# Twelve expert weight slots instead of six, ten filled in the router, and squares added on VectorE

## The reference, cut to what matters

```python
def swiglu(xb, wg, wu, wd):
    return (jax.nn.silu(xb @ wg) * (xb @ wu)) @ wd

def hier_moe(h, lp):
    ...
    eid = grp[:, None].astype(jnp.int32) * MOE_EXPERTS_PER_GROUP + top_i.astype(jnp.int32)
    ...
    order = jnp.argsort(flat_e)
    se, st, sw = flat_e[order], flat_t[order], w.reshape(-1)[order]
    counts = jnp.bincount(flat_e, length=MOE_EXPERTS)
    ...
    yb = lax.map(expert_block, (xin, block_e)).reshape(n_rows, d)
    return jax.ops.segment_sum(yb[dest] * sw[:, None].astype(h.dtype), st, num_segments=t)

def _rms_norm(x, w):
    xf = x.astype(jnp.float32)
    y = xf * lax.rsqrt(jnp.mean(xf * xf, axis=-1, keepdims=True) + EPS)
    return (y * w.astype(jnp.float32)).astype(x.dtype)

def _swiglu(h, w1, w3, w2):
    return (jax.nn.silu(h @ w1) * (h @ w3)) @ w2
```

## Time and profile before

| | |
|---|---|
| median of 3 runs | 2530.34 us (2528.55 to 2536.39) |
| profiled execution | 2529.34 us, span 2528.0, mean granted clock 0.992 |
| busy, share of the span | PE 96%, DVE 56%, ACT 41%, POOL 12% |
| chain that ended last | PE 74%, DVE 11%, DMA 10%, ACT 4%; of DMA's, 6% is the expert tile `pair<-in_ed` |
| weight tiles of experts | 192 of 1024 KB, 9.6 to 11.8 us from issue to landing at the median |
| DMA rate in the slices of the experts | 398 to 417 GB/s |
| waits of PE, whole span | 14.6 us ahead of line 739, 11.1 ahead of 1291 |

### The profile page before, as it was taken

How to read it: one execution, slowest core, us unless ns; L and a number is a source line. 1 busy time by engine, 2 the same in 40 slices (tenths; PEclk the granted TensorE clock), 3 DMA queues, 4 the chain that set the end, 5 groups by cost and what they waited for, 6 DMA issues and landing times.

```text
span 2528.0 us, 30627 instructions
## 1 busy us (share of the span) xinstructions
PE 2426.0 (96%) x12294; PEld 1876.3 (74%) x12294; DVE 1409.5 (56%) x2043; ACT 1036.8 (41%) x1570; POOL 301.5 (12%) x256
## 2 busy tenths in 40 slices
PE   6999999999999989999999889999999999999999
PEld 4877868687877767666666678888888777888887
DVE  3676776768636676544555565334443667543442
ACT  2424333343536346544555553223343546422221
POOL 0010112112222311111111120000013000000000
PEclk9999999999999989999999999999999999999999
DMA  7324243333446259999999823232232111323322
GB/s 273 113 75 167 79 155 121 116 118 103 139 152 237 103 201 373 417 407 398 404 407 403 351 92 103 81 117 90 85 124 75 43 42 59 109 76 107 101 79 79
DMA packets 115747, 428.10 MB, mean 169 GB/s; under 512 B 16320, under 2 KB 30912, under 8 KB 89872
## 3 DMA queue, kind: packets, MB, share of 16 engines
q1 hardware_dynamic: 91488, 377.42, 41.0%
q10 hardware_dynamic: 12960, 25.17, 2.7%
q0 software_dynamic: 11152, 23.49, 2.7%
HBM read 411.60 MB, written 31.72 MB: 175 GB/s over the span
## 4 chain that ended last, share of the span: by engine, by line
PE 74%; DVE 11%; DMA 10%; ACT 4%; issue 1%; POOL 0%; SPq 0%; ACTq 0%; POOLq 0%; DVEq 0%
PE bank L739 18%; PE bank L741 18%; PE bank L740 18%; DMA pair<-in_ed 6%; PE bank L1291 3%; PE bank L1292 2%; PE bank L1293 2%; DVE HLB L280 2%; PE bank L1348 2%; DVE HLB L417 2%; ACT HLB L406 1%; PE bank L1654 1%; DMA raw<-in_wxbc 1%; DVE XGl L3002 1%; PE bank L1677 1%
## 5 line engine op out<-in xcount | busy, mean ns | idle before, releaser
L417 DVE TENSOR_TENSOR HLB<-raw,HLB 128x1024 fp32r<-128x1024 f32 (+1 forms) x286 | 346.7, 1215 | 382.1 <-ACT HLB L406 381.8
L739 PE MATMUL bank<-HTh,HLB 128*128 128x512 f32 (+1 forms) x1358 | 542.5, 400 | 14.6 <-DVE HLB L417 11.0
L741 PE MATMUL bank<-HTh,HLB 128*128 128x512 f32 (+1 forms) x1358 | 531.0, 391 | 0.0
L740 PE MATMUL bank<-HTl,HLB 128*128 128x512 f32 (+1 forms) x1358 | 528.2, 389 | 0.0
L406 ACT ACTIVATE HLB<-raw 128x1024 fp32r<-128x1024 f32 (+1 forms) x294 | 289.4, 991 | 298.9 <-PE bank L741 270.9
L739 PEld LDWEIGHTS bank<-HTh,HLB 128*128 128x128 f32 x1358 | 257.1, 189 | 97.3 <-issue 27.4
L740 PEld LDWEIGHTS bank<-HTl,HLB 128*128 128x128 f32 x1358 | 257.3, 189 | 54.0 <-issue 1.9
L741 PEld LDWEIGHTS bank<-HTh,HLB 128*128 128x128 f32 x1358 | 257.3, 189 | 53.8
L280 DVE TENSOR_TENSOR HLB<-pair,HLB 128x1024 fp32r<-128x1024 f32 x136 | 159.6, 1221 | 110.2 <-ACT HLB L271 109.4
L271 ACT ACTIVATE HLB<-pair 128x1024 fp32r<-128x1024 f32 x136 | 135.9, 1062 | 120.4 <-DMA pair<-in_ed 108.3
L741 PE MATMUL bank<-FAh,HLB 128*128 128x512 f32 x352 | 139.2, 396 | 0.0
(11 more groups left out here) (606 smaller groups left out, 4356.8 us busy)
## 6 DMA issues: line engine op xcount, KB each, us to landing
pair<-in_ed SPq DMA_DIRECT2D x64, 1024.0 KB, 11.3
raw<-in_f SPq DMA_DIRECT2D x120, 512.0 KB, 3.4
pair<-in_eg SPq DMA_DIRECT2D x47, 1024.0 KB, 9.6
raw<-in_eu SPq DMA_DIRECT2D x47, 1024.0 KB, 11.3
raw<-in_wada SPq DMA_DIRECT2D x40, 512.0 KB, 4.2
raw<-in_eg SPq DMA_DIRECT2D x17, 1024.0 KB, 11.6
pair<-in_eu SPq DMA_DIRECT2D x17, 1024.0 KB, 11.8
raw<-in_wxbc SPq DMA_DIRECT2D x24, 512.0 KB, 4.1
```

Source lines behind the costliest of these rows:

```text
L417: self.nc.vector.tensor_tensor(lo, raw, hi.bitcast(F32), ALU.subtract).then_inc(*self.w_lo.next(n))
L739: mm(bank, ah, bh, start=(start and i == 0), stop=False)
L740: mm(bank, ah, bl, start=False, stop=False)
L741: ins = mm(bank, al, bh, start=False, stop=(stop and i == n - 1))
```

## The change

The slots become twelve: beside the six of before, four `ht_pair` in the halves HTh and HTl of the normed input (no longer read once the token rows are written), `tmp_pair` in TMP[2] to TMP[5], `dec_pair` in the buffer of the decays, from which WROW moves out. A table of turns tells a tile's slot: the first five tiles go to slots 0, 1, 2, 3, 10, then the turn is 0, 1, 6, 7, 8, 9, 11, 4, 5, 2, 3, 10. SP loads two tiles as before, goes on to seven once the mean square ("square", 1) and MU_STD ("std") are done, and to twelve once PE has passed the token rows ("rows"); numbers 10 and 11 are of expert 2 and wait for `eids`.

The first four parts are split early: ACT makes two hi halves at the router's start and two behind the offsets' copies, and GpSimd, not DVE, makes their lo halves (`lo_early`, signal `x_first`). DVE's `moved(6)`, `moved(7)`, `normed(0)`, `normed(1)` come behind the slots' indices. PE's rank matmuls come ahead of the first four `offset`, its weight row and slots matmuls ahead of the first `turn_in`, which fills with one constant matmul, not three. PICK waits in addition for the last tile in `dec_pair`. The next block's first loads wait for the last tiles in slots 0, 1 and 4, now 185, 186 and 180 in place of 186, 187 and 190. ACT writes the squares of "n1" to four buffers of TMP by turns, DVE adds them, and `pe_rms` comes right behind the first product.

```diff
+        for n in range(6 * len(small)):
+            self.at.append(turns[0][n] if n < len(turns[0]) else turns[1][(n - len(turns[0])) % len(turns[1])])
+            self.before.append(had.get(self.at[n], -1))
+            had[self.at[n]] = n
+        self.last_in = had
...
     def raw(self, n):
-        return self.slots[n % len(self.slots)]
+        return self.slots[self.at[n]]
+
+    def rest(self, h):
+        return self.lo_first.when(h) if self.lo_first and h < FIRST_PARTS else self.w_lo.when(h)
+
+    def free(self, sp, n):
+
+        if n in self.first:
+            sp.wait_ge(*self.rest(self.first[n] + 1))
+        elif n >= 0:
+            sp.wait_ge(*self.pe_out.when(("tile", n)))
...
+    def lo_early(self, pool):
+
+        while self.lo_made < FIRST_PARTS:
+            h = self.lo_made
+            hi, lo, raw, _n = self.part(h)
+            pool.wait_ge(*self.w_hi.when(h))
+            self.nc.gpsimd.tensor_tensor(lo, raw, hi.bitcast(F32), ALU.subtract).then_inc(*self.lo_first.next(h))
+            self.lo_made += 1
...
+        ht_pairs = [place(f"ht_pair{i}", [128, 2048], off=HT_AT + 2048 * i) for i in range(4)]
+        tmp_pair = place("tmp_pair", [128, 2048], off=TMP_AT + 1024)
+        dec_pair = place("dec_pair", [128, 2048], off=DEC)
...
-                        keep_busy(bank, 3)
+                        keep_busy(bank, 1)
...
-            turn_in(0)
             if S.kept:
                 pe_weight_row()
                 pe_slots()
+            turn_in(0)
...
         def act_router():
+            ring.hi(act, "wr", 0, itself=True)
+            act.wait_ge(*pe_out.when(("used", ring.start_of("wr", 0))))
+            tiles.hi(act, 2)
             act.wait_ge(*pe_out.when("rcol"))
...
+            tiles.hi(act, FIRST_PARTS)
             act.wait_ge(*act_out.when("rcol"))
...
-                if i == 2:
-                    ring.hi(act, "wr", 0, itself=True)
-                    act.wait_ge(*pe_out.when(("used", ring.start_of("wr", 0))))
-                    tiles.hi(act, 4)
...
-                act_square("n1", k)
+                if k > 3:
+                    act.wait_ge(*dve_out.when(("sumsq", "n1", max(k - 4, 1))))
+                activation(TMP[k % 4][:, :], XT[:, k, :], ACT.Square).then_inc(*act_out.next(("sq", "n1", k)))
...
-            tiles.lo(dve, 4)
-            moved(6)
-            moved(7)
-            for k in range(2):
-                normed(k)
...
+                tiles.free(dve, tiles.last_in[11])
...
+            for k in range(1, 8):
+                dve.wait_ge(*act_out.when(("sq", "n1", k)))
+                if k > 1:
+                    dve.wait_ge(*dve_out.when(("sumsq", "n1", k - 1)))
+                tensor_tensor(SQ[:, :], TMP[0][:, :] if k == 1 else SQ[:, :], TMP[k % 4][:, :], ALU.add).then_inc(
+                    *dve_out.next(("sumsq", "n1", k)))
...
+            tiles.lo_early(pool)
...
         tiles.load(sp, 2)
         sp.wait_ge(*pe_out.when(("used", ring.start_of("wo", 7))))
-        tiles.load(sp, 4)
+        sp.wait_ge(*pe_out.when(("square", 1)))
+        sp.wait_ge(*act_out.when("std"))
+        tiles.load(sp, 7)
+        sp.wait_ge(*pe_out.when("rows"))
+        tiles.load(sp, 12)
...
         for i in (0, 1, 4):
-            n = max(n for n in range(len(tiles.order)) if n % len(tiles.slots) == i)
-            sp.wait_ge(*x_lo.when(tiles.first[n] + 1))
+            tiles.free(sp, tiles.last_in[i])
```

More of the change, by code:

```diff
@@ L246, in load @@
             n = self.loaded
-            before = n - len(self.slots)
-            if before in self.first:
-                sp.wait_ge(*self.w_lo.when(self.first[before] + 1))
-            elif before >= 0:
-                sp.wait_ge(*self.pe_out.when(("tile", before)))
+            self.free(sp, self.before[n])
             source = self.source(*self.order[n])
@@ L254, in load @@
             self.nc.sync.dma_start(self.raw(n).rearrange("p (k n) -> p k n", k=k), source).then_inc(
[L255 removed]
+                *self.loads[self.at[n]].next(n))
             self.loaded += 1
@@ L267, in hi @@
             hi, _lo, raw, n = self.part(h)
-            act.wait_ge(*self.loads[n % len(self.slots)].when(n))
+            act.wait_ge(*self.loads[self.at[n]].when(n))
             if h >= NHL:
@@ L292, in whole @@
         n = self.tile_of[(j, name, a)]
-        pe.wait_ge(*self.loads[n % len(self.slots)].when(n))
+        pe.wait_ge(*self.loads[self.at[n]].when(n))
         return n, self.raw(n).rearrange("p (k n) -> p k n", k=k)
@@ L1217, in pe_router @@
                 rows(2, q)
-            for i in range(2):
-                for q in range(2):
-                    offset(i, q)
             bank = psum.take(pe, "rank")
@@ L1226, in pe_router @@
             psum.give("rank", dve_out, "rk")
+            for i in range(2):
+                for q in range(2):
+                    offset(i, q)
             for q in range(2):
@@ L3025, in dve_experts @@
                 dve_slots()
+                for k in (6, 7):
+                    moved(k)
+                for k in range(2):
+                    normed(k)
             for j in range(len(blocks)):
```

41 lines of the change are left out of this document (22 added, 19 removed).

## The result

The changed kernel takes **2513.2 us** (median of 5 runs, 2512.26 to 2518.85), the kernel before 2533.2 (2528.55 to 2537.41) in the same measurement: a ratio of **0.993**, 95% interval 0.9918 to 0.9942. That is 20.0 us between the medians, where the prediction had 18.5, and 2513.2 lies within its range. The interval of the ratio reaches from 14.7 to 20.8 us, and the profiled execution, of 2515.06 us, has a span of 2513.8, only 14.2 less than the span before. So that the two numbers agree to 1.5 us is in part luck.

What follows compares the result with a forecast made beforehand. The weight queue was taken to bound the expert stage. From the profiled 2529.34 us, 10.9 (last tile earlier), 1.5 (seam) and 6.0 (squares) come off: 2510.9, or 2511.8 us against the median; range 2501 to 2523.

Steps and rivals of the forecast that it cites:

- P: Start of PE's first expert matmul, forecast at 925.7 us, 4.4 later than the 921.35 before.
- The hold: Router, ahead of the rank matmuls: GpSimd's lo-half operations hold up DVE's mask chain by 6.6 us (0 to 10.4).
- The clock: Router, behind the rank wait: PE's clock falls after standing 6.4 us, adding 2.5 us (0 to 3.4).
- The last write of token rows: Router: only 0.8 us (0 to 2) was added, for tiles 7 to 9 in the stretch around the gather.
- They run while the gather flies and cost nothing: Router: PE's weight row and slots matmuls, now ahead of the transposes, add 0 us to P.
- From P to the last landing: Expert stage: last weight tile lands at P+500.5 (P+515.7 before), with tile 22 at P+38.9, then 2.70 us a tile.
- Ten early tiles: Weight queue: how many of ten are early decides little, as the queue stands some 5.5 us before tile 22.
- Seam: Behind the experts: the next block's first loads go out ahead of expert 30's scatter, saving 1.5 us (0 to 3).
- Squares: Next block's mean square: VectorE adds the squares, PE's wait and low clock go, saving 6.0 us (3.45 to 6.3).
- No hold-up: Rival, router: DVE isn't held up by GpSimd, P is 917.6, total 2503.7 us; chance 0.20.
- Gathers behind the tiles: Rival, expert stage: more queued tiles delay gathers and scatters, so PE lags, total 2519.5 us; chance 0.20.
- A slower queue: Rival, weight queue: more slots slow the tiles; at 2.85 us a tile the total is 2537.3 us; chance 0.07.

Runs made afterwards that it cites:

- n1pool: Changed kernel with the next block's squares summed on GpSimd again and pe_rms back inside PE's long product: 2522.6 us, ratio 0.9961.
- seam: Changed kernel with the next block's first loads held again until tile 190 is split: 2517.8 us, ratio 0.9950.
- fill: Changed kernel with eight constant matmuls on PE ahead of its wait for the rank masks: 2507.7 us, ratio 0.9905.
- seven: Changed kernel with tiles 7 to 9 loaded behind the first gather, seven tiles early in place of ten: 2518.6 us, ratio 0.9949.
- dvelo_six: Changed kernel with the four early splits on DVE at other places, tile 6 in an ht_pair slot, six tiles early: 2506.5 us, ratio 0.9895.
- best1: dvelo_six with first turn_in ahead of weight row and slots matmuls, five constant matmuls before first transposes, tiles 6 to 9 right behind the gather's landing: 2502.7 us.
- eight: Changed kernel with eight slots in place of twelve, ten tiles early all the same: 2529.9 us, ratio 0.9988.
- later: Changed kernel with GpSimd's four early splits waiting until DVE has made the rank masks: 2510.6 us, ratio 0.9913.
- best2: best1 with two constant matmuls on PE ahead of the last expert's down matmuls: 2498.6 us, ratio 0.9875.

## Why the prediction was right, and where it was not

**What bounds the kernel.** Right: the weight queue, before and after. PE is busy for 271.79 of 280 us now and is no bound; it waits 0.5 us for a raw tile and 8.0 for halves from 1120 to the end of the experts.

**P.** Wrong by 14.1 us, of which 1.3 lie ahead of the router; counted from MU_STD 12.8, and 9.8 and 10.3 in n1pool and seam. The hold was sized right (6.5 for 6.6), and so was the order of events. The size is luck in part: two and a half operations of GpSimd were a choice between 0 and 10.4 us, for a chain of two-input operations, and of the four that were held three have one input. Three steps failed.
- The clock. I gave it 2.5 us, 3.4 at the most, from ten us behind another wait. It lasted from the rank to the blocks matmuls, all of the path: 22.8 us in place of 12.2 in this profile, 18.9 to 19.7 in five others with the same router, 11.9 in fill. Less the 12.2 of the forecast the term is 6.7 to 10.6 us.
- The last write of token rows. The sum had 0.8 us for the early tiles beside the gather. They stood beside the write ahead of it, which took 8.8 us for 3.1, and the gather came 7.0 us behind the blocks matmuls, not 3.7 (3.6 in seven, without those tiles). The prediction followed the queue past the gather's issue and not past what the gather waits for.
- "They run while the gather flies and cost nothing", of the weight row and slots matmuls. They, at the low clock, and the wait ahead of them take the time from 926.6 to 934.6, which the late write hid here; without that write, dvelo_six has P 11.5 us behind its gather, best1 9.1.

**From P to the last landing.** Wrong by 9.0 us, to the other side. Tile 22 came at P+37.7 for P+38.9. The 170 tiles from there to the last landing took 453.8 us (977.44 to 1431.22), not 461.6: 2.67 us a tile with the first landing, and in the chain 31.4 us a pair (six pairs from 1163.46 to 1351.95) where I held on to 32.4. In n1pool the 170 tiles take 454.1 us, but tile 22 comes at P+40.6, so there it is 5.8 us, not 9.0: the 7.8 of the rate repeat, the 1.2 at tile 22 don't. The assumption that the rate doesn't depend on depth was called the one that would be most wrong, and it was, with a sign that the prediction did not price: it had a slower queue as a rival and no faster one. The dips that it could have read were in the trace of before, in the rate by slices, behind a share of 1.01.

The two errors cancelled: 12.8 late at P, 9.0 gained behind it. Neither was foreseen, so that the sum came out is luck. The last landing was 5.0 us later than predicted, of which 1.3 again lie ahead of the router.

**Ten early tiles.** That fewer would cost nothing isn't contradicted by seven's profile, and not shown by its times. The stand of the queue that it rests on is there: DMA's share is 0.11 from 974 to 976 in the changed kernel, 1.00 in seven. eight shows that ten early ones without the slots bring little.

**Seam.** Forecast 1.5, up to 3. From the down matmuls to the transposes of the results (1456.86 before, 1448.55 now) 2.5 us were gained. The mechanism, the scatter beside the loads, was right: 6.28 us before, 2.6 now. What the traces show of its worth is 0.9 to 1.9 us: 0.9 of the 2.5 are the wait for the results (2.46 before the transposes at 1456.86, 1.56 now), 1.9 in seam, and the other 1.6 are the way from the down matmuls to PICK, 9.06 us before and 7.5 now, a clock that differs between kernels with the same instructions there.

**Squares.** Forecast 6.0. The long product starts at 1497.12 with no wait. By the same matmuls in both traces (the last one of the first product, and the fifteenth of the long one: 1503.85 and 1514.39 before, 1496.55 and 1500.72 now) it gained 10.54 - 4.17 = 6.4 us, and undoing it costs 6.3 in n1pool's profile. Right in its parts; that the medians lie 7.8 to 9.4 us apart isn't explained.

**Rivals.** No hold-up: refuted, by the rows and by later. Gathers behind the tiles: refuted, 7.6 and 9.5 us at a depth of ten. A slower queue: refuted, it is faster.

## What to carry to other kernels

A wait of TensorE is priced with what follows it: here 8.1 us of standing cost some 7 to 11 more, and the cheapest cure was work that nobody needs, put into the wait. A DMA busy share of 1.0 doesn't say that the transfers are as fast as they can be; read the rate by slices, and where it dips, more slots may bring more than the head start that they were meant for. A small operation with a busy neighbour on GpSimd and a small write behind large reads, both on the way to the critical step, cost more than their own length. And before 3 us in a stage are explained, look for another profile with the same instructions there.

## What the runs showed of the hardware

- GpSimd's operation of 128x1024 held up DVE's copies, casts, scalings, scans and two-input operations of 0.17 to 0.29 us for up to 2.4 us, the length of GpSimd's. DVE's searches for maxima (lines 2856 and 2859) beside the second split stayed at 0.37 and 0.09 to 0.16 us.
- The rate of one queue of 1 MB loads from HBM: 405, 412 and 422 GB/s at six, eight and twelve slots, at the same busy share.
- A gather's time to landing does not depend on how many tiles are queued ahead (7.3 and 9.7 us with some four, 7.6 and 9.5 with ten), while a tile's goes from some 10 to 12 us to 23 to 28.
- A 512 KB write took 2.6 to 3.1 us alone and 8.8 beside three 1 MB loads issued from 0.7 us ahead of it on.
- The same wait of 2.6 to 2.7 us ahead of the last down matmuls was followed by a low clock in some profiles (0.76 over the next seven us in the kernel before and in seam, 0.55 in fill) and not in others (1.00 in the changed kernel). The same instructions with a wait of 1.64 and of 1.79 us ahead of the first transposes had a low clock behind it in best1 (0.65 over the first five us from P) and none in best2 (1.00).
- The identical work ahead of the router ended anywhere within 6.2 us (884.1 to 890.3).
